# A two-layer hybrid decoder step on one core: one block without barriers between phases, first products in the tail of the phase ahead, and a reordered first phase

## What is computed

```
for l in range(2):
    h = rms_norm(x) * norm_g[l]
    q, k, v, gate_a, f, u, v_b, gate_b, m_a, m_b = split(h @ w_in[l])
    q, k = qk_norm(q), qk_norm(k)
    a = softmax(q k^T * scale + D) v        # D: sums of log sigmoid(f)
    s = w_s[l] @ norm(gelu(v_b)) + b_s[l]   # per chunk of 128 rows
    a = (a * silu(gate_a)) @ w_proj_a[l]
    b = (gelu(u) * s * silu(gate_b)) @ w_proj_b[l]
    x = x + (sigmoid(m_a) * a + sigmoid(m_b) * b) @ w_out[l]
```

## Time and profile before

| | |
|---|---|
| runs | 2104.22, 2105.61, 2107.80 us |
| median | 2105.61 us |
| profiled execution | 2106.33 us |
| its span | 2104.6 us |
| mean granted clock of TensorE | 0.972 |
| busy: TensorE, its weight loads | 1935.8 us (92%), 1778.3 us (84%) |
| busy: VectorE, ScalarE, GpSimd | 969.4, 673.7, 515.1 us |

### The profile page before, as it was taken

The page is one execution under the profiler, slowest core; times in us unless marked ns, Lnnn a source line. Parts: engine busy times, 40 slices in busy tenths (PEclk is TensorE's granted clock), DMA queues, the critical chain, the costliest instruction groups (busy, mean ns, idle before and its releaser), DMA issues. The chain is left out here.

```text
span 2104.6 us, 31060 instructions
## 1 busy us (share of the span) xinstructions
PE 1935.8 (92%) x11188; PEld 1778.3 (84%) x11188; DVE 969.4 (46%) x2304; ACT 673.7 (32%) x1487; POOL 515.1 (24%) x517
## 2 busy tenths in 40 slices
PE   2889999999897999999988998999998799999998
PEld 1879888999876889998868998989997688899986
DVE  3345656554155324445434465555532633354431
ACT  3233434444232322213213343343442332221120
POOL 3432333333011112211115132333310121131110
PEclk9999999999998999999999999999999999999999
DMA  4231231223223322533323212131322142226141
GB/s 125 50 97 45 57 84 51 80 56 108 63 54 94 97 85 74 176 110 111 128 58 74 79 50 80 49 94 51 87 63 68 43 142 79 73 75 205 66 160 50
DMA packets 217227, 178.39 MB, mean 85 GB/s; under 512 B 50196, under 2 KB 189988, under 8 KB 217076
## 3 DMA queue, kind: packets, MB, share of 16 engines
q1 hardware_dynamic: 217076, 176.41, 28.7%
HBM read 131.65 MB, written 44.71 MB: 84 GB/s over the span
## 5 line engine op out<-in xcount | busy, mean ns | idle before, releaser
L75 PE MATMUL bank<-keep_hhi,at_fhi 128*128 128x384 f32 (+1 forms) x768 | 261.7, 341 | 16.4 <-ACT at_th L850 16.4
L76 PE MATMUL bank<-keep_hlo,at_fhi 128*128 128x384 f32 (+1 forms) x768 | 255.3, 332 | 0.0
L77 PE MATMUL bank<-keep_hhi,at_flo 128*128 128x384 f32 (+1 forms) x768 | 255.1, 332 | 0.0
L75 PE MATMUL bank<-keep_hhi,bw_whi 128*128 128x384 f32 (+1 forms) x576 | 196.7, 341 | 10.5 <-PEq L2157 10.5
L75 PE MATMUL bank<-aw_whi,keep_hhi 128*128 128x384 f32 (+3 forms) x576 | 200.1, 347 | 4.3 <-PEq L2157 4.3
L76 PE MATMUL bank<-aw_wlo,keep_hhi 128*128 128x384 f32 (+3 forms) x576 | 197.7, 343 | 0.0
L77 PE MATMUL bank<-aw_whi,keep_hlo 128*128 128x384 f32 (+3 forms) x576 | 197.4, 343 | 0.0
L76 PE MATMUL bank<-keep_hlo,bw_whi 128*128 128x384 f32 (+1 forms) x576 | 190.0, 330 | 0.0
L77 PE MATMUL bank<-keep_hhi,bw_wlo 128*128 128x384 f32 (+1 forms) x576 | 189.7, 329 | 0.0
L896 ACT ACTIVATE at_prob<-at_prob,at_nmx 128x128 f32<-128x128 f32 (+7 forms) x128 | 99.5, 777 | 279.0 <-DVE at_nmx L1084 278.9
L1093 DVE TENSOR_TENSOR at_ptlo<-bank,at_pthi 128x512 fp32r<-128x512 f32 x192 | 106.1, 553 | 155.5 <-ACT at_pthi L906 155.5
(11 more groups left out here) (255 smaller groups left out, 4410.8 us busy)
## 6 DMA issues: line engine op xcount, KB each, us to landing
at_stage<-in_w_in SPq DMA_DIRECT2D x152, 128.0 KB, 2.5
mg_gate<-gates SPq DMA_DIRECT2D x32, 544.0 KB, 5.4
gates<-at_th SPq DMA_DIRECT2D x64, 192.0 KB, 2.3
br_stage<-in_w_in SPq DMA_DIRECT2D x40, 256.0 KB, 3.2
at_stage<-in_w_in SPq DMA_DIRECT2D x48, 192.0 KB, 2.5
at_decay<-ncum SPq DMA_DIRECT2D x16, 512.0 KB, 3.8
br_k<-in_cache_k SPq DMA_DIRECT2D x32, 256.0 KB, 2.9
br_v<-in_cache_v SPq DMA_DIRECT2D x32, 256.0 KB, 2.9
```

Of the source, the lines that this page charges most:

```text
L75: nc.tensor.matmul(out, sh, mh, start=start and i == 0, stop=False)
L76: nc.tensor.matmul(out, sh, ml, start=False, stop=False)
L77: last = nc.tensor.matmul(out, sl, mh, start=False, stop=stop and i == n - 1)
```

## The change

1. There is one block for all phases. Each engine raises a counter of its own when it is through a phase (`pe_through`, `act_through`, ...; four of them behind a `drain`, SP when its stores have landed). At a phase's start ScalarE, VectorE, GpSimd and SP wait for all five counters (`all_through`). GpSimd then clears the semaphores of the phase three back and raises `cleared_through`; from the first spatial phase on TensorE waits for that one (`g.sem.cleared(pe)`), and otherwise for the semaphores of its data and banks. In branches, VectorE and ScalarE wait at a new step M of the plan, ahead of piece 3; VectorE's memsets have moved into it.
2. First products of a phase are in the tail of the one ahead: tiles 0 and 1 of the first pair (`first_tile`) at the end of rows and of output in layer 0, pieces 0 to 2 of branches (`first_piece`) in spatial around the last two gatings. The head's split for output is done in merge (`head_lo`).
3. All eight units of spatial's value projection are split in attention. X comes two tiles behind Z, no longer one. The constants of attention are issued by SP ahead of the gate. Banks are dealt out anew, so that consecutive phases don't meet in one.
4. `constants_phase` is part of `rows_phase`; there the square runs three tiles ahead, mean(t+2) stands behind hn(t), GpSimd's weight split is one tile later, and the gain is loaded behind x of tile 0.

Core of the diff (indentation ignored):

```diff
+def first_tile(nc, g, t, out, ks):
+    r = slice(t * P, (t + 1) * P)
+    for k in ks:
+        last = three(nc, out[:, 0:WID], [(g.h_hi[:, k, r], g.h_lo[:, k, r], g.a_whi[:, k, :], g.a_wlo[:, k, :])],
+                     k == 0, k == KT - 1)
+    return last
+def all_through(eng, g):
+    eng.wait_ge(g.pe_through, g.phases)
+    eng.wait_ge(g.act_through, g.phases)
+    eng.wait_ge(g.dve_through, g.phases)
+    eng.wait_ge(g.pool_through, g.phases)
+    eng.wait_ge(g.sp_through, g.phases)
...
 rows_phase, ScalarE
+        square(2)
             for t in range(NT):
-                square(t + 2)
+            square(t + 3)
                 act.wait_ge(tr_r, t + 1)
 rows_phase, VectorE
                 n = ROWS[t]
-                mean(t + 2)
                 dve.wait_ge(rs_r, t + 1)
...
                                                gain[0:n, :], ALU.mult, ALU.mult).then_inc(hn_r, 1)
+            mean(t + 2)
 rows_phase, TensorE, behind the transposes
+        pe.drain().then_inc(g.pe_through, 1)
+        pe.wait_ge(w_lo, KT)
+        for t in range(2):
+            first_tile(nc, g, t, g.bank[1 - t], range(KT)).then_inc(z_first, 1)
 attention_plan
-        if t:
-            plan.append(("X", 0, t - 1))
+        if t >= 2:
+            plan.append(("X", 0, t - 2))
 attention_phase, SP
-            for u in range(NST):
-                load_w(u)
             for i, src in enumerate((g.q_norm_g, g.k_norm_g)):
...
+        all_through(sp, g)
+        for u in range(NST):
+            load_w(u)
 spatial_phase, TensorE, the end
+        first_piece(0)
             gating(NT - 2)
+        pe.wait_ge(g2_r, NT - 1)
+        first_piece(1)
             gating(NT - 1)
+        pe.wait_ge(g2_r, NT)
+        first_piece(2)
+        pe.drain().then_inc(g.pe_through, 1)
 branches_plan and branches_phase, VectorE
+        if i == 3 and part == 0:
+            plan.append(("M",))
...
+            if s[0] == "M":
+                all_through(dve, g)
             nc.vector.memset(selb[:, :, :], 1.0).then_inc(fills, 1)
 merge_phase, ScalarE
+        for k in range(KT):
+            act.wait_ge(m_b, max(3 * k + 2, 3 * (NG + k // 2) + 3))
+            nc.scalar.activation(g.h_hi[:, k, head], g.m[:, k, head], ACT.Copy, scale=0.5).then_inc(k_hi, 1)
 output_phase, TensorE, the end in layer 0
+            pe.wait_ge(aw_lo, KT)
+            pe.wait_ge(y_ready, NT - 1)
+            first_tile(nc, g, 0, g.bank[1], range(KT)).then_inc(z_first, 1)
+            pe.wait_ge(y_ready, NT)
+            first_tile(nc, g, 1, g.bank[0], range(KT // 2))
                 transposes(NT - 1)
+            pe.drain().then_inc(g.pe_through, 1)
+            first_tile(nc, g, 1, g.bank[0], range(KT // 2, KT)).then_inc(z_first, 1)
 Semaphores
+    def clear(self, pool):
+        if len(self.order) >= 3:
+            for r in self.numbers(self.order[-3]):
+                pool.sem_clear(r)
+            self.count += 1
+            pool.sem_inc(self.done, 1)
+    def cleared(self, pe):
+        if self.count:
+            pe.wait_ge(self.done, self.count)
```

More of the change, by code:

```diff
@@ L600, in attention_plan @@
         else:
-            for u in range(PRE_SPATIAL):
+            for u in range(KT):
                 put(n + 2 + 2 * u, ("Y", u))
@@ L1573, in branches_phase @@
     own_v, fills = S("own"), S("fills")
+    unit_lo, first_free = g.unit_lo, g.first_free
+    g.merge_units = [(w_lo_v if u % 2 else w_lo_p, (NU + u - PRE_BRANCH) // 2 + 1) for u in range(PRE_MERGE)]
+    g.c_lo, g.o_r, g.piece_free = c_lo, o_r, (g2_r, len(pieces))
     def wait_split(eng, u):
@@ L1959, in merge_phase @@
+def merge_phase(nc, l, g):
     R = Region(nc, "me", g.free_rows)
[L1960 removed]
+    S = g.sem("m", l)
     NW, NST, NG = 6, 3, 4
@@ new lines, with __init__, __call__, named @@
+class Semaphores:
+    def __init__(self, nc, done):
+        self.nc, self.done = nc, done
+        self.of, self.open, self.count = {}, {}, 0
+        self.order = []
+    def __call__(self, letter, l):
+        key = (letter, l)
+        if key not in self.of:
+            self.of[key], self.open[key] = {}, ExitStack()
+        def named(name):
+            if name not in self.of[key]:
+                self.of[key][name] = self.open[key].enter_context(self.nc.semaphore(f"{letter}{l}_{name}"))
+            return self.of[key][name]
+        return named
+    def numbers(self, key):
+        nums = sorted(s.num for s in self.of[key].values())
+        firsts = [n for n in nums if n - 1 not in nums]
+        return [range(a, next(b for b in range(a, 999) if b not in nums)) for a in firsts]
+    def clear(self, pool):
[7 more added lines that the diff above has]
+            pe.wait_ge(self.done, self.count)
+    def release(self):
+        if len(self.order) >= 3:
+            self.open[self.order[-3]].close()
+    def left(self):
+        return [r for key in self.order[-2:] for r in self.numbers(key)]
@@ L2144, in program, with phase @@
     with ctx:
[L2145 to L2164 removed]
+        g.pe_through, g.act_through, g.dve_through, g.pool_through, g.sp_through, done = (
+            ctx.enter_context(nc.semaphore(f"{x}_through")) for x in ("pe", "act", "dve", "pool", "sp", "cleared"))
+        g.sem = Semaphores(nc, done)
+        g.phases = 0
+        def phase(letter, l, build, *args):
+            g.sem.order.append((letter, l))
+            build(*args)
+            g.sem.release()
+            g.phases += 1
         g.end = nc.sbuf_base + nc.sbuf_bytes_remaining
```

2956 lines of the change are left out of this document (1515 added, 1441 removed).

## The result

| | before | after |
|---|---|---|
| runs, us | 2103.23 to 2107.80, median 2104.91 (4) | 2066.44 to 2073.18, median 2070.66 (4) |
| ratio of the runs | | 0.9834, 95% interval 0.9814 to 0.9854 |
| profiled execution, us (span) | 2106.33 (2104.6) | 2073.18 (2071.4) |
| mean granted clock | 0.972 | 0.974 |
| TensorE busy | 1935.8 us | 1940.2 us |

The kernel is 34.3 us faster, 1.7%. The forecast was 2061 with 2048 to 2078 around it; the sum had 44.7 us, so 10 us of it did not come. The profiled execution is the slowest of the four, 2.5 us over their median.

The account below looks back on a forecast made before the run. TensorE works 92% of the span, so only its standing still and low clock can shrink; terms of 21.9, 5.7, 1.2, 10.4, 1.0, 0.4 and 4.1 sum to 44.7, 2105.61 - 44.7 = 2061 us, range 2048 to 2078 (0.80).

Parts of the forecast that it names:

- The row loop, -21.9: Opening row loop: reordering cuts 6 us a tile to 3.1, first product at 38.7 against 60.59; -21.9 us.
- Into attention 0, -5.7: Start of attention 0: the 3.70 us wait for GpSimd's at_qn is covered, half clock behind it goes; -5.7 us.
- Ring (b): Row loop's x buffer: hn, load of x, square, copy, lo, hn again; 9.0 us for three tiles.
- Attention to spatial, -0.6: Seam into spatial: TensorE still waits for `cleared_through`, only the barrier itself goes; -0.6 us in each layer.
- merge, -0.5: Seam into merge: first product waits for the gate and `c_lo`, only barrier time goes; -0.5 us, twice.
- Spatial tail and entry of the branches, -5.2 a layer: Pieces 0 to 2 fill spatial's holes; a new wait at step D and low clock leave -5.2 us a layer.
- Output, -0.2: Seam into output: taking the head's copies in merge shortens the wait for keep_hlo; -0.2 us, twice.
- Output 0 into attention 1, -4.1: Start of attention 1: first product starts when GpSimd's last split ends, 4.3 sooner, less 0.2 for order; -4.1 us.
- The signs that were named: Trace signs: before spatial near 5 us, before D 8 to 9, then 0.50 under 10, no hole before first X.
- Rival A: Seams: TensorE enters on data alone, so the gate costs nothing; 2024 us, chance 0.07 for all below 2048.
- Rivals B, C, D: B: wait at step D eats branches' gain, above 2078, 0.09; C: slower, clock stays low, 0.02; D: nothing gained, 2105, 0.02.
- ring (c): Row loop, an engine's own work per tile: ScalarE 2.8 us, VectorE 2.7, GpSimd 2.5.

Follow-up runs that it names:

- e11: Changed kernel with both row-loop edits undone (mean(t+2) ahead of hn(t) again, square two tiles ahead): 2088.87 us, ratio 0.9915.
- e7: Kernel before with only the two row-loop edits (mean(t+2) behind hn(t), square three tiles ahead): 2085.55 us, ratio 0.9912.
- e12: Changed kernel with the X transposes one tile behind Z again: 2075.25 us, ratio 0.9855.
- e3: Changed kernel; attention 1's first product, in output 0's tail, does seven of eight steps before waiting for GpSimd's last weight split: 2064.65 us, ratio 0.9792.
- e10: Changed kernel with e1, e2, e3 and e9 together: 2019.32 us, ratio 0.9582.
- e2: Changed kernel; TensorE waits for the clearing of one phase earlier, and output waits for merge's last reads of its banks: 2050.98 us, ratio 0.9733.
- e9: e2 with spatial's `sg_wb` loads ahead of the bias loads, ScalarE and VectorE each waiting for their own: 2038.10 us, ratio 0.9673.
- e1: Changed kernel with VectorE's memsets out of step M, ahead of and right behind piece 0's product with br_sc: 2051.96 us, ratio 0.9740.
- e8: Changed kernel with pieces 0 to 2 of branches behind the gate again, memsets still behind them: 2090.96 us, ratio 0.9927.
- e4: Changed kernel with e1, e2 and e3 together: 2030.32 us, ratio 0.9632.

## Why the prediction was right, and where it was off

- **The row loop, -21.9: right** (-21.8), with its ring (e11) and its place in the order (e7); that it agrees to 0.1 us is in part luck. The parts missed by more, in both directions. hn(0) ended at 12.95 and not at 12.2: the gain landed in 5.4 us and not 7.0, and what hn(0) stood behind was mean(1), which waits for the load of x(1) (6.4 us). The eight tiles took 23.5 us and not 24.8, since the first step was 1.7. From the last transposes to the first product it was 2.3 and not 1.7. Ring (b), sized at 9.0 us for three tiles, took 9.1 to 9.6: loads took 1.2 to 1.7 us more than 3.7, while the steps behind them were shorter (VectorE's lo begins 0.6 us behind ScalarE's copy, not 1.1). The bound of -17 for a tile of 3.8 us should have been -16.3.
- **Into attention 0, -5.7: right in size** (-5.8), half wrong in its reason. The prediction gave the covered 3.70 us to the distance of X and to the constants together; e12 shows that layer 0 did not need the distance.
- **Attention to spatial, -0.6, and merge, -0.5: right** (-0.7, -0.6, -0.5, -0.6). The gate is as good as a barrier, as the prediction had it from the wait for `cleared_through`.
- **Spatial tail and entry of the branches, -5.2 a layer: right in its mechanism, sized too well** (-3.1 and -2.9). Up to the gate it came out as forecast. From the middle of spatial on, in layer 0, the changed kernel is 25.2 us ahead. Beside that the last store is issued 2.0 us sooner (630.76 against 657.92; forecast 1.9), and SP is past the gate 2.8 sooner (forecast 2.6). "release 13.1" was 13.95, since the load of `spatial` took 3.05 us and not 2.6 and the evacuation a little longer: D is 7.6 us sooner and not 8.3. "6.8 us at 0.50 cost about 3.1": the grant stayed at 0.50 until 655.8, 8.6 us behind the start of D, and 4.0 us were lost there. The last half microsecond went at the start of spatial, where 5.5 us of work fell into the low stretch and not 4.5. In layer 1 the start of spatial gave 0.4 us, D is 6.7 us sooner, and 4.1 are lost behind it.
- **Output, -0.2: wrong in sign.** The seam went from 3.54 to 3.78 us in layer 0 and from 3.42 to 3.88 in layer 1. VectorE's last head copy ends at 941.8 and TensorE begins at 942.48: the copies moved into merge saved less than the prediction took for them. The rest of the rows "output" and "end" is not the seam: 0.6 us in layer 0 and 1.3 in layer 1 went inside merge, whose low stretch held 6.1 us of work in both layers, where before it was 4.8 and 3.2. In layer 1 the low stretch behind the seam into output gave 1.0 back (3.4 us long and not 6.8).
- **Output 0 into attention 1, -4.1: half of it came** (-1.9). The first product started where it was expected, 4.3 us sooner against its surroundings (offset -32.6, ahead of it -28.3), and at the last X of the first pair 3.3 were left (1145.15 against 1113.61); a wait of 1.06 us for VectorE's `at_klo` (at 1106.80), which the kernel before does not have, lies in between. The step that failed is "From there to tile 2 the work stays as it was" with its "one low stretch of the clock", and that nothing was counted behind tile 2: over the 56 us from that X on the changed kernel had 17.0 us at 0.50 in three stretches, the one before 10.2 in two, and the offset fell by 1.6. Why the grant fell more often there is not shown. e3 shows what the term left lying besides: most of the hole itself need not have been there.
- **What no term had**: 2.6 us were lost in the middle of attention 0, where nothing was changed. The window at 242.8 shows 8.30 us of work at 0.50; in the kernel before the stretch at that place was 3.4 us. The first costs 4.2 us, the second 1.7, and the difference is the loss. It belongs to the execution more than to the change: of the twelve experiments' traces eleven have 3.4 us at this place, and only e10 has 10.2 again.
- **The signs that were named.** D waited 9.15 and 8.74 us (8 to 9 forecast), TensorE 4.9 and 5.0 ahead of spatial (near 5), the low clock behind D lasted 8.6 and 8.9 us (under 10), and there was no hole ahead of the first X.
- **Rival A** had 2024 for a TensorE without the gate. The change itself did not do it. Made to (e2), it reached 2051, and 2038 once the loads behind the gate were in order (e9). The seams of merge and output were as the rival said, the one of spatial was bound by loads.
- **Rivals B, C, D** did not come. The loop ran at 2.9, the wait at D took part of the branches' gain and not all, and no low stretch around D was longer than 13.7 us in the changed kernel or 20.5 in any experiment.

## What to carry to other kernels

A barrier replaced by "everyone waits for everyone's counter" keeps all of the barrier's cost but the last 0.5 to 0.7 us here; what brings time is to find the engine that needs only its data and let it off, and then to see which load was issued behind the old barrier, since that is what is late next. When work is moved ahead of a gate, look at what stood between the gate and the moved work: here four memsets of 3 us came to stand behind 8 us of evacuation, and cost 10 us a layer (e1) of the 13 that the moved products bring with the memsets out of the way. And in a loop shared by five engines write down the ring that each order makes: two small edits of order, either of which does most of it alone, were worth 17 to 21 of 34 us.

## What the hardware showed that was not expected

- The granted clock was 0.50 for 20.5 us around the start of the branches in e7 and in e8, longer than any stretch of the kernel before (13.7), and for 23.9 us in the row loop in e3, e4, e7 and e12 (20.5 in e2), where the changed kernel itself had 1.00 at about the same load. TensorE was busy 10.74 of 18 us in e3, the first row, and 11.16 of 18 in the changed kernel, the second:

```profile
20.00:38.00 18.00, 10.74 (x48) 8.74 (x48) 16.02 (x23) 12.89 (x26) 8.47 (x11) 0.50 0.56 132
```

```profile
20.00:38.00 18.00, 11.16 (x49) 8.77 (x48) 16.14 (x22) 13.32 (x28) 8.37 (x11) 1.00 0.47 130
```

  In the row loop it costs nothing that shows, since TensorE waits there for hn: the first product comes at 37.8 to 39.4 us in these five, at 38.83 in the changed kernel. What decides between the two grants is not shown. The Trainium skill (TensorE: Matmul & The Clock Gate, Seeing it yourself) tells of a gate seen stuck low for over 50 us; no run here shows that.
- Beside VectorE's hn GpSimd's tiny pow takes 1.52 us. In the changed order only the second pow (11.78) begins during an hn and takes 1.57; all others begin beside other work of VectorE or none and take 0.55 (14.82, 18.32 and 21.50 in the trace). So the new order also took load from GpSimd, which the prediction's ring (c) had at 2.5 us a tile. The other way round, the one hn that took 2.54 us in place of 1.28 (31.58) lies beside two of GpSimd's weight splits.
- Eight loads of 2 KB cost SP 2.77 us to issue and eight of 32 KB 5.18 (the two rows of e9). That is 0.3 and 0.6 us each, and the 512 KB of an x tile cost 0.33 (the row at 14.71): many small loads in a row are paid for at the issuing engine, whatever they carry, and what stands last in such a row decides.
